# The first layer's MLP: half of its fc1 groups as block products (Strassen-Winograd), fc2 after every four fc1 tiles, side jobs moved forward

## The chip, the cores and the metric

The kernel runs on one core of a Trainium2 chip. The metric is the device time of one execution, in microseconds (us). TensorE (PE) multiplies, VectorE (DVE) and ScalarE (ACT) work element by element, GpSimd (POOL) does a few such operations, and SyncE (SP) sends most of the weight transfers.

## The reference

Two transformer-like blocks of two layers each, in float32. The part in question is the MLP of the first layer of the first block. It runs for 512 tokens and for 256 context tokens, with the same weights; the kernel does both as 768 columns.

```python
def _sq_relu_mlp(h, w1, w2):
    a = jnp.maximum(h @ w1, 0)
    return (a * a) @ w2
...
        x = _layer_norm(DEEPNORM_ALPHA * x + g2 * _sq_relu_mlp(h, w_fc1[l], w_fc2[l]), ln2_g[l], ln2_b[l])
```

D_MODEL is 1024 and the hidden size 4096. `g2` is one of six modulation vectors of a layer, a product of a condition with a 1024 x 6144 matrix.

## The kernel before, in words

Each engine has one queue of instructions, written out by hand in Python; what stands in it is done in that order, and semaphores tie the queues together. Activations lie with features on the partitions and tokens along the row.

**Precision by parts.** Every float32 matrix product is three matmuls: high weight by high operand, low weight by high operand, high weight by low operand. So each weight tile (128 x 1024, 512 KB) that has landed is split: ScalarE copies the high part (`act_split`, L590) and VectorE subtracts it (`dve_split`, L622). High parts have NS = 3 places, so the copy for tile a waits until TensorE is through with tile a - 3; landed tiles and low parts have a ring of NR = 4 slots. `act_tiles(key)` and `dve_tiles(key)` do the splits up to the tile two after `key`.

**The first layer's MLP** (`mlp`, `pe_mlp`, `act_mlp`, `dve_mlp`) has fc1 with 32 tiles of 128 hidden features and fc2 with 32 tiles too, in four rounds: eight fc1 tiles, then the eight output tiles of fc2 for these eight. A tile is 24 pairs of matmuls with 512 and 256 columns (`pe_dense`, L866 and L870), and goes in turn to one of two PSUM banks of 1024 columns, ps[0] and ps[1]. An fc1 tile is evicted in four steps: ScalarE's Relu (L1252, which frees the bank), VectorE's square (L1276), ScalarE's high part (L1254), VectorE's low part (L1279). An fc2 tile is added to the residual by VectorE (`dve_add_gated`, L924), which frees the bank.

**Jobs.** Beside this MLP the kernel makes the modulation vectors of the next two layers (`modulation`). It has 128 jobs, each a 512 KB tile of the modulation matrix in one of NM = 3 buffers, multiplied and summed on VectorE (L731), and four changes of condition (two transposes' banks copied by ScalarE, L721). They are dealt evenly over 64 steps, one step behind each tile; a step has two or three jobs. In ScalarE's queue a step is, for each job, a wait until VectorE has done it and the send (L691) that refills its buffer.

**The later MLPs** (`eighths`, `quarters`, with 512 tokens) already use block products. In `eighths` the hidden features come in eight groups of four tiles; the first is plain, the others are seven products of half size in place of eight (Winograd's form of Strassen). A product is 24 matmuls of 256 columns (L1378). VectorE also makes the sums of the weight blocks (L600) and of the products (L1546). The fc2 of each group follows it at once; a transfer tile of fc2 there holds two outputs of four blocks each, and its banks are four of 512 columns. The ring has XR = 4 more slots from the second layer's MLP on.

```python
                act_tiles((name, "evict", q, m) if e != 0 else fc1(name, 0, 1))
                ACTQ.wait_ge(*made(key))
```

These lines of `act_mlp` set which weight copies stand ahead of a tile's Relu; the mark ("evict", q, m) lies right behind tile m. In `act_eighths` it is

```python
                    act_tiles(fc1(name, 0, min(m + 2, 3)))
                    evict(m)
```

## Time and profile before

| | |
|---|---|
| median of 3 runs | 3000.74 us (2996.26 to 3006.47) |
| profiled execution, its own time | 3000.01 us |
| span of its trace | 2998.7 us |
| PE busy | 2843.8 us (95%) |
| DVE busy | 1877.8 us (63%) |
| ACT busy | 1197.6 us (40%) |
| POOL busy | 340.6 us (11%) |
| moved by DMA | 315.98 MB, mean 105 GB/s |

Each engine's busy time is given with its share of the span. PE runs nearly always, so the other engines matter where PE waits for them. The first layer's MLP takes the span's stretch from about 514 to 1070 us.

### The profile page before, as it was taken

The page shows a single profiled execution, that of the slowest core. Times are in us where ns is not written, and L with a number is a line of the kernel's source. Part 1 is how long each engine was busy: PE and PEld are TensorE (multiplying, and loading weights), DVE is VectorE, ACT ScalarE, POOL GpSimd, SP SyncE. Part 2 cuts the span into 40 slices and gives each one's busy share as a digit, 9 for nine tenths or more (in the row PEclk, how much of TensorE's full clock was granted, in tenths as well). Part 3 has the DMA queues.
Part 4 walks back from the last instruction along what each step waited for, and adds up shares of the span by engine and source line. Part 5 has one row for each costly group of instructions (what it writes and reads, how often), then busy time and mean ns, then how long its engine had stood idle before and what let it go on. Part 6 is the DMA issues. An engine that isn't in the chain of part 4 may idle for free. (4 is left out here: it accounts for less than half of the span.)

```text
span 2998.7 us, 43305 instructions
## 1 busy us (share of the span) xinstructions
PE 2843.8 (95%) x17474; PEld 2305.1 (77%) x17474; DVE 1877.8 (63%) x2790; ACT 1197.6 (40%) x1963; POOL 340.6 (11%) x371
## 2 busy tenths in 40 slices
PE   7999998999999989999899998998889999899998
PEld 6766667888888867766688886776667999678896
DVE  3656544656565646665687765646736788567765
ACT  4245443412122252554443555212643444344443
POOL 2022220300000030321301002000510000110000
PEclk9999999999999999999999999998999999999999
DMA  7222001556565511001232331322024555412331
GB/s 282 78 98 80 8 22 43 169 196 210 171 209 183 194 57 51 8 15 57 89 106 81 110 113 57 102 64 63 1 89 131 167 182 168 138 59 90 106 106 64
DMA packets 88495, 315.98 MB, mean 105 GB/s; under 512 B 9991, under 2 KB 12295, under 8 KB 88040
## 3 DMA queue, kind: packets, MB, share of 16 engines
q1 hardware_dynamic: 59040, 213.94, 22.3%
q10 hardware_dynamic: 29256, 99.26, 9.9%
q8 instruction: 140, 2.29, 0.3%
q14 instruction: 59, 0.48, 0.1%
HBM read 311.06 MB, written 2.10 MB: 104 GB/s over the span
## 5 line engine op out<-in xcount | busy, mean ns | idle before, releaser
L866 PE MATMUL bank<-t 128*128 128x512 f32 x4064 | 1011.0, 360 | 25.5 <-ACT t L1172 7.7
L866 PEld LDWEIGHTS bank<-t 128*128 128x128 f32 x4064 | 672.9, 190 | 164.4 <-issue 41.4
L590 ACT ACTIVATE t<-t 128x1024 fp32r<-128x1024 f32 x410 | 431.0, 1055 | 761.0 <-PE bank L870 263.9
L622 DVE TENSOR_TENSOR t<-t 128x1024 fp32r<-128x1024 f32 x410 | 508.3, 1243 | 332.3 <-ACT t L590 328.1
L870 PE MATMUL bank<-t 128*128 128x512 f32 x2032 | 607.6, 359 | 8.3 <-POOL t L1181 7.6
L870 PEld LDWEIGHTS bank<-t 128*128 128x128 f32 x2032 | 336.3, 190 | 73.7 <-POOL t L1181 11.9
L1399 PE MATMUL bank<-t 128*128 128x512 f32 x1024 | 309.6, 398 | 1.2 <-ACT t L1469 1.0
L1378 PEld LDWEIGHTS bank<-t 128*128 128x128 f32 x2352 | 281.4, 188 | 1.9 <-issue 0.8
L1378 PE MATMUL bank<-t 128*128 128x256 f32 x2352 | 282.0, 281 | 0.0
L1399 PEld LDWEIGHTS bank<-t 128*128 128x128 f32 x1024 | 190.8, 189 | 55.3 <-issue 5.7
L731 DVE SCALAR_TENSOR_TENSOR t<-t 128x1024 f32<-128x1024 f32 x176 | 209.3, 1222 | 4.6 <-DMA t<-in_mod 4.5
L1404 PE MATMUL bank<-t 128*128 128x512 f32 x512 | 187.4, 396 | 0.0
L1898 POOL TENSOR_SCALAR t<-t 128x768 f32<-128x768 f32 (+3 forms) x160 | 125.7, 788 | 522.0 <-DVE t L1866 522.0
L924 DVE SCALAR_TENSOR_TENSOR t<-bank,t 128x512 f32<-128x512 f32 (+1 forms) x128 | 81.5, 664 | 148.2 <-PE bank L870 131.0
L1697 PE MATMUL bank<-t 64*128 64x384 f32 (+2 forms) x768 | 136.9, 475 | 16.1 <-ACT t L1796 5.2
L1841 DVE TENSOR_REDUCE t<-bank 128x1 f32<-128x768 f32 (+1 forms) x120 | 96.6, 845 | 86.9 <-PE bank L1706 65.8
L1786 ACT ACTIVATE t<-bank 128x384 f32<-128x384 f32 (+1 forms) x160 | 73.6, 460 | 172.3 <-PE bank L1714 171.9
L1714 PEld LDWEIGHTS bank<-t 128*128 128x128 f32 x784 | 86.8, 142 | 58.2 <-issue 29.1
L1714 PE MATMUL bank<-t 128*128 128x128 f32 x784 | 121.9, 284 | 9.5 <-DVE t L1852 6.7
L1796 ACT ACTIVATE t<-bank,t 128x768 f32<-128x768 f32 (+3 forms) x160 | 124.1, 780 | 14.0 <-DVE t L1841 8.0
L992 ACT ACTIVATE t<-t 128x512 f32<-128x512 f32 (+1 forms) x64 | 43.8, 684 | 214.2 <-DVE t L924 132.6
L1592 DVE SCALAR_TENSOR_TENSOR t<-bank,t 128x512 f32<-128x512 f32 x128 | 93.5, 746 | 48.1 <-PE bank L1404 47.8
(363 smaller groups left out, 3385.3 us busy)
## 6 DMA issues: line engine op xcount, KB each, us to landing
t<-in_mod ACTq DMA_DIRECT2D x176, 512.0 KB, 4.3
t<-in_l0fc SPq DMA_DIRECT2D x64, 512.0 KB, 4.1
t<-in_l1fc SPq DMA_DIRECT2D x64, 512.0 KB, 3.6
t<-in_s0fc SPq DMA_DIRECT2D x64, 512.0 KB, 3.7
t<-in_s1fc SPq DMA_DIRECT2D x64, 512.0 KB, 3.6
t<-in_mod SPq DMA_DIRECT2D x48, 512.0 KB, 4.5
t<-in_mixin SPq DMA_DIRECT2D x24, 512.0 KB, 3.6
t<-in_l0in SPq DMA_DIRECT2D x12, 512.0 KB, 3.7
```

The costliest lines, as they stand in the source:

```text
L590: act.activation(high_of(key), landed_of(key), ACT.Copy).then_inc(*up("act_whi", a))
L622: dve.tensor_tensor(low_of(key), landed_of(key), high_of(key).bitcast(F32), ALU.subtract).then_inc(*up("dve_wlo", a))
L731: dve.scalar_tensor_tensor(x, x, 1.0, sil[:, :], ALU.mult, ALU.mult, accum_out=modt[L][:, j, s:s + 1]).then_inc(*up("dve_job", (name, n)))
L866: pe.matmul(acc.ap[:, o:o + m], w[:, ws], Hh[:, k, o:o + m], start=k == order[0] and w is hi, stop=False)
L870: ins = pe.matmul(acc.ap[:, o:o + m], hi[:, ws], Hl[:, k, o:o + m], start=False, stop=k == order[-1])
L1378: ins = pe.matmul(dst, w[:, ws], x, start=pair == 0 and k == 0 and w is hi and x is high, stop=pair == 1 and k == 3 and x is low)
L1399: pe.matmul(banks[s].ap, w[:, ws], Ah[:, k, :], start=first and w is hi, stop=False)
L1404: ins = pe.matmul(banks[s].ap, hi[:, ws], Al[:, k, :], start=False, stop=last)
L1697: ins = pe.matmul(places[side][:, 512 * r + o:512 * r + o + m], g["q"][side](c), g["k"][side][:, k0:k0 + m], start=r not in begun, stop=last)
L1714: ins = pe.transpose(turns[r].ap[:, P * b:P * b + P], p[:, P * i:P * i + P], mat("ident"))
L1796: act.activation(keys_of(p, g), scores_of(ps[side], g), ACT.Exp, bias=row[:, 7:8], accum_out=row[:, 3:4]).then_inc(*ps[side].freed((tag, u ...
L1898: pool.tensor_scalar(x, x, stat(u, side)[:, 7:8], 1.0, ALU.mult, ALU.mult).then_inc(*up("pool_prob", (tag, u, side)))
```

## The change

The function `mlp` with its three queues goes, and the first layer's MLP uses `eighths`, which now takes a number of plain groups G, the token ranges and jobs. G is 4 for this MLP and 1 for the two others that use it. The last four groups are block products: 24 matmuls of 384 columns each, with three banks of 1024 columns. Fc2 follows every four fc1 tiles. A weight tile of fc2 holds two outputs of four blocks. There are now eight rounds, and so twice as many additions to the residual. The jobs are dealt over 128 steps: 24 steps in each plain group (three behind each tile), 8 in each block group, behind the fc2 tiles alone. The four additional ring slots come with this MLP. In `s0` and elsewhere the functions are only renamed.

```diff
-                self.slot[key], self.slot_after[key] = NR + a - G, ("l1out", 1)
+                self.slot[key], self.slot_after[key] = NR + a - G, ("l0out", 1)
...
+PLAIN_GROUPS = {"l0": 4, "l1": 1, "s0": 2, "s1": 1}
...
-                pe_step, act_step, dve_step, pool_all = modulation(name, sb(s, [P, 1024]), jobs, 2, 62)
...
+                *steps, pool_all = modulation(name, sil, jobs, 2, 126)
...
+    PRODUCT_BANKS = {NT: (0, 1, 2, 3, 0, 2, 3), T: (2, 0, 1, 2, 1, 2, 0)}
+    OUT_BANKS = {NT: (1, 0, 2, 3), T: (1, 0)}
...
+    def steps_beside(G, Q, m):
+
+        return range(24 * Q + 3 * m, 24 * Q + 3 * m + 3)
+
+    def steps_behind(G, Q, j):
+
+        return range(24 * Q + 12 + 3 * j, 24 * Q + 15 + 3 * j) if Q < G else range(16 * G + 8 * Q + 2 * j, 16 * G + 8 * Q + 2 * j + 2)
...
             if j == 0:
                 for s in range(2):
                     PEQ.wait_ge(*banks[s].claim(out_of(name, Q, 2 * j + s)))
-                for ks in ((1, 3), (0, 2)) if Q else ((0, 1), (2, 3)):
+                for ks in ((1, 3), (0, 2)) if Q >= G else ((0, 1), (2, 3)):
...
+        places = {key: fours[m % 4] if n == NT else ps[m % 4 % 3] for m, key in enumerate(first)}
...
-            if Q == 0:
+            if Q < G:
                 for m in range(4):
-                    act_tiles(fc1(name, 0, min(m + 2, 3)))
-                    evict(m)
+                    act_tiles(fc1(name, 4 * Q + min(m + 2, 3)))
+                    evict(Q, m)
+                    if step:
+                        for s in steps_beside(G, Q, m):
+                            step(s)
...
-                act_tiles(fc2_pair(name, Q, j))
-                if Q == 0:
+                act_tiles(fc2(name, Q, j))
+                if Q == G - 1:
                     for t in ((0, 1), (2,), (3,), ())[j]:
                         operand_high(t)
+                if step:
+                    for s in steps_behind(G, Q, j):
+                        step(s)
...
+                if Q == 0:
+                    dve_tiles(fc1(name, 1))
+                    for t in range(4):
+                        operand(t)
                 for m in range(4):
-                    dve_tiles(fc1(name, 0, min(m + 2, 3)))
-                    evict(m)
+                    dve_tiles(fc1(name, 4 * Q + min(m + 2, 3)))
+                    evict(Q, m)
+                    if step:
+                        for s in steps_beside(G, Q, m):
+                            step(s)
```

How ScalarE's queue stands in an fc1 round of this MLP, away from its ends. L590 (L579 in the changed kernel) is a weight copy, L1252 (L1402) the Relu, L1254 (L1407) the high part, L691 (L680) the sends of jobs. Before, two tiles:

```order
L590 ACTIVATE t<-t 128x1024 [waits s_pe_tile,s_tile_in2]
L1252 ACTIVATE t<-bank 128x768 [waits s_pe_tile]
L1254 ACTIVATE t<-t 128x768 [waits s_dve_asq]
L691 DMA t<-in_mod 128x1024 [waits s_dve_job] x3
L590 ACTIVATE t<-t 128x1024 [waits s_tile_in3]
L1252 ACTIVATE t<-bank 128x768 [waits s_pe_tile]
L1254 ACTIVATE t<-t 128x768 [waits s_dve_asq]
L691 DMA t<-in_mod 128x1024 [waits s_dve_job] x2
```

In the changed kernel, the four fc1 tiles of plain group 1:

```order
L579 ACTIVATE t<-t 128x1024 [waits s_pe_tile,s_tile_in2]
L579 ACTIVATE t<-t 128x1024 [waits s_pe_tile,s_tile_in3]
L579 ACTIVATE t<-t 128x1024 [waits s_pe_tile,s_tile_in0]
L1402 ACTIVATE t<-bank 128x768 [waits s_dve_alo]
L1407 ACTIVATE t<-t 128x768 [waits s_dve_asq]
L680 DMA t<-in_mod 128x1024 [waits s_dve_job] x3
L579 ACTIVATE t<-t 128x1024 [waits s_pe_tile,s_tile_in1]
L1402 ACTIVATE t<-bank 128x768 [waits s_dve_alo]
L1407 ACTIVATE t<-t 128x768 [waits s_dve_asq]
L680 DMA t<-in_mod 128x1024 [waits s_dve_job] x3
...
L1402 ACTIVATE t<-bank 128x768 [waits s_dve_alo,s_pe_tile]
L1407 ACTIVATE t<-t 128x768 [waits s_dve_asq]
```

Three weight copies now stand ahead of a group's first Relu, one ahead of the second and none ahead of the other two; only the last Relu still has a wait of its own for TensorE.

TensorE's queue at the last fc1 matmuls of such a round and the first of fc2. Before:

```order
L870 MATMUL bank<-t 128x512
L870 MATMUL bank<-t 128x256
L866 MATMUL bank<-t 128x512 [waits s_ps1_read,s_act_ahi,s_dve_wlo,s_act_whi]
L866 MATMUL bank<-t 128x256
```

In the changed kernel:

```order
L859 MATMUL bank<-t 128x512
L859 MATMUL bank<-t 128x256
L1328 MATMUL bank<-t 128x512 [waits s_ps0_read,s_ps1_read,s_act_ahi,s_dve_wlo,s_act_whi]
L1328 MATMUL bank<-t 128x256
```

The first fc2 matmul waited for one bank, and now waits for two, ps[0] being the one that the group's fourth tile has just filled.

## Rows read from the trace of the kernel before

**Rows 1.** Stretches of 100 us: busy of each engine, granted clock, DMA share, GB/s.
```profile
600.00:700.00 100.00, 100.00 (x574) 87.28 (x573) 59.39 (x86) 20.92 (x22) 0.00 (x0) 1.00 0.61 197
...
900.00:1000.00 100.00, 100.00 (x573) 87.35 (x572) 60.68 (x83) 24.83 (x27) 0.00 (x0) 1.00 0.58 184
```
**Rows 2.** Waits of TensorE, 514 to 1050 us: total us, times, longest.
```profile
PE bank L866 <- ACT t L1172: 2.8, 1, 2.8
PE bank L870 <- POOL t L1181: 1.2, 1, 1.2
```
**Rows 3.** Timeline of VectorE, two additions: start, us, line, idle before and its releaser.
```profile
613.20 1.14 DVE L924 SCALAR_TENSOR_TENSOR t<-bank,t 128x512 f32<-128x512 f32 x2 [3.35 <-PE bank L870]
...
621.60 1.14 DVE L924 SCALAR_TENSOR_TENSOR t<-bank,t 128x512 f32<-128x512 f32 x2 [2.59 <-PE bank L870]
```
**Rows 4.** The chain that ended last, one block group of the last MLP.
```profile
2728.09 20.00 PE bank L1378 x168
```
**Rows 5.** Timeline of VectorE, one fc1 tile with three jobs.
```profile
582.23 0.96 DVE L1279 TENSOR_TENSOR t<-t 128x768 fp32r<-128x768 f32 x1 [0.91 <-ACT t L1254]
583.11 1.22 DVE L731 SCALAR_TENSOR_TENSOR t<-t 128x1024 f32<-128x1024 f32 x1
...
585.40 1.22 DVE L731 SCALAR_TENSOR_TENSOR t<-t 128x1024 f32<-128x1024 f32 x1
...
588.21 1.23 DVE L622 TENSOR_TENSOR t<-t 128x1024 fp32r<-128x1024 f32 x1 [1.58 <-ACT t L590]
589.35 0.95 DVE L1276 TENSOR_TENSOR t<-t 128x768 f32<-128x768 f32 x1
591.21 0.96 DVE L1279 TENSOR_TENSOR t<-t 128x768 fp32r<-128x768 f32 x1 [0.91 <-ACT t L1254]
```
**Rows 6.** Groups of instructions, 536 to 1036 us: busy, mean ns, idle before and releasers.
```profile
L731 DVE SCALAR_TENSOR_TENSOR t<-t 128x1024 f32<-128x1024 f32 x125 | 148.2, 1223 | 2.6 <-DMA t<-in_mod 2.5
...
L590 ACT ACTIVATE t<-t 128x1024 fp32r<-128x1024 f32 x60 | 63.5, 1061 | 272.9 <-PE bank L870 143.1 <-DVE t L731 129.3 <-issue 0.4
```
**Rows 7.** Timeline of ScalarE in the same tile.
```profile
587.04 1.06 ACT L590 ACTIVATE t<-t 128x1024 fp32r<-128x1024 f32 x1 [4.84 <-DVE t L731]
588.01 0.79 ACT L1252 ACTIVATE t<-bank 128x768 f32<-128x768 f32 x1
```
**Rows 8.** Timelines of ScalarE and TensorE, the second MLP's plain group.
```profile
1474.38 0.57 ACT L1464 ACTIVATE t<-bank 128x512 f32<-128x512 f32 x1
...
1477.02 0.58 ACT L1464 ACTIVATE t<-bank 128x512 f32<-128x512 f32 x1
...
1479.39 0.58 ACT L1464 ACTIVATE t<-bank 128x512 f32<-128x512 f32 x1
...
1481.53 1.67 PE L1399 MATMUL bank<-t 128*128 128x512 f32 x6 [1.03 <-ACT t L1469]
```
**Rows 9.** Timelines of ScalarE, VectorE and GpSimd, the stage's start.
```profile
514.10 19.49 ACT L1172 ACTIVATE t<-t 128x512 fp32r<-128x512 f32 x32 [4.64 <-DVE t L1124]
...
534.86 1.80 DVE L622 TENSOR_TENSOR t<-t 128x1024 fp32r<-128x1024 f32 x1 [8.30 <-ACT t L590]
...
535.58 15.15 POOL L1185 TENSOR_SCALAR t<-t 128x768 f32<-128x768 f32 x8
```
**Rows 10.** Timeline of VectorE, a late job and the norm's shifts.
```profile
1011.48 1.23 DVE L731 SCALAR_TENSOR_TENSOR t<-t 128x1024 f32<-128x1024 f32 x1 [1.22 <-DMA t<-in_mod]
...
1012.69 0.96 DVE L1009 TENSOR_TENSOR t<-t 128x768 f32<-128x768 f32 x1
1013.57 0.95 DVE L1011 TENSOR_TENSOR t<-t 128x768 f32<-128x768 f32 x1
```
**Rows 11.** DMA issues of the page: queue, count, size, median us to landing.
```profile
t<-in_mod ACTq DMA_DIRECT2D x176, 512.0 KB, 4.3
```
**Rows 12.** Timeline of TensorE after a wait, and the granted clock of the stretch around it.
```profile
1858.89 2.05 PE L866 MATMUL bank<-t 128*128 128x512 f32 x4 [6.58 <-DVE t L3419]
...
1855.00:1860.00 5.00, 1.11 (x3) 0.94 (x4) 2.63 (x4) 4.45 (x7) 2.54 (x2) 0.50 0.03 10
1860.00:1865.00 5.00, 5.00 (x13) 3.85 (x12) 1.52 (x4) 1.94 (x4) 4.64 (x8) 0.50 0.00 0
```

More of the change, by code:

```diff
@@ L287, in quarters_order, with mlp_order @@
     t.mark((name, "end"))
-def eighths_order(t, name):
+def mlp_order(t, name):
     t.tile((name + "fc1", 0))
     t.tile((name + "fc1", 1), 1)
-    for m in range(2, 4):
-        t.tile((name + "fc1", m))
     for Q in range(8):
-        if Q:
+        if Q < PLAIN_GROUPS[name]:
+            for m in range(0 if Q else 2, 4):
+                t.tile((name + "fc1", 4 * Q + m))
+        else:
             t.quad(name + "fc1", Q)
@@ L299, in eighths_order @@
             t.tile((name + "fc2", 4 * Q + j))
-    t.mark((name, "end"))
-def mlp_order(t, name):
-    t.tile((name + "fc1", 0))
-    t.tile((name + "fc1", 1), 1)
-    for q in range(4):
-        for m in range(NK):
-            if 8 * q + m > 1:
-                t.tile((name + "fc1", 8 * q + m))
-            t.mark((name, "evict", q, m))
-        for m in range(NK):
-            t.tile((name + "fc2", 8 * q + m))
     t.mark((name, "end"))
@@ L1305, in eighths @@
-    def eighths(L, name, N, after, centered, make_h, columns, beside=None, weights=None):
-        n, half = NT, 256
+        half = n // 2
         keys = [out_of(name, 7, m) for m in range(NK)]
@@ L1323, in eighths @@
             cells = modw[:, 0:2, :].rearrange("p a (b n) -> p (a b) n", b=2) if L == 1 else sb(S, [P, 4, n])[:, :, :]
-            M = Norm(after, LAT, [space[:, i, :] for i in range(4)], centered, updated_at(keys, after, centered), weights)
+            sil = sb(S, [P, 1024]) if jobs else None
+            M = Norm(after, ranges, [space[:, i, :] for i in range(4)], centered, updated_at(keys, after, centered), weights)
             begin_stage()
@@ L1398, in high @@
                 for w in (hi, lo):
-                    pe.matmul(banks[s].ap, w[:, ws], Ah[:, k, :], start=first and w is hi, stop=False)
+                    for o, m, _ in ranges:
+                        pe.matmul(banks[s].ap[:, o:o + m], w[:, ws], Ah[:, k, o:o + m], start=first and w is hi, stop=False)
             def low(s, k, last):
@@ L1403, in low @@
                 ws = slice(512 * s + P * k, 512 * s + P * k + P)
-                ins = pe.matmul(banks[s].ap, hi[:, ws], Al[:, k, :], start=False, stop=last)
+                for o, m, _ in ranges:
+                    ins = pe.matmul(banks[s].ap[:, o:o + m], hi[:, ws], Al[:, k, o:o + m], start=False, stop=last)
                 if last:
@@ L1443, in pe_eighths, with act_eighths @@
                     beside(4 * Q + j)
+                if step:
+                    for s in steps_behind(G, Q, j):
+                        step(s)
         pe_norm_step(M, 7, acc_of[keys[0]].after(keys[0]))
[L1445 to L1446 removed]
+        if n == NT:
+            for bank in fours:
+                PEQ.wait_ge(*bank.after(bank.order[-1]))
         pe_tiles((name, "end"))
[L1449 to L1450 removed]
+    def act_eighths(name, G, htag, n, Hh, Tr, T3, Th, Ah, cells, M, beside, step):
+        half = n // 2
         def operand_high(t):
@@ L2877, in pe_quads @@
             PEQ.wait_ge(*bank.claim((name, "quads")))
-        first = [fc1(name, 0, m) for m in range(NK)]
+        first = [fc1(name, m) for m in range(NK)]
         pe_dense(first[0:2], Hh, Hl, hh, hl, LAT, dict(zip(first, fours)))
```

448 lines of the change are left out of this document (185 added, 263 removed).

## The prediction

> **What bounds the kernel now.** I read the span and the stretches first. The core is in the first MLP from about 514 to 1070 us, and inside it TensorE has no free moment: 100.00 of 100 us busy in each stretch, at full clock [rows 1]. The list of waits says the same: from 514 to 1050 us TensorE waited twice, 4.0 us together, both at the stage's start [rows 2]. So this stage costs what its matmuls cost, and a cut in matmul columns comes out at the end as long as nobody makes TensorE wait. The question is whether VectorE and ScalarE keep ahead in the new order.
>
> One tile takes 8.40 us: two successive second-layer additions on VectorE, each started by the end of its tile, stand 8.40 us apart [rows 3]. It has 24 pairs of a 512- and a 256-column matmul, so 350 ns a pair. In the later block stage 168 matmuls of 256 columns take 20.00 us, 119 ns each [rows 4]. A 512-column one is then 231 ns, and a 384-column one, halfway, 175 ns; by the 256-column row times 1.5 it would be 179 ns at most.
>
> Then the other engines. One tile with three jobs on VectorE [rows 5]: low part, three jobs at 1.15 us, a wait of 1.58 us for ScalarE's weight copy, weight split, square, a wait of 0.91 us, low part. From one low part's start to the next are 8.98 us, against a tile of 8.40; with two jobs it is 7.83. It fits today because the mean is 2.2 jobs a tile. ScalarE is not busy but it is tied: of its idle time before weight copies 129.3 us end with a job of VectorE [rows 6], since in its queue the sends that refill the job buffers stand ahead of the copy and wait for the jobs. It comes to the weight copy at 587.04, 0.5 us after the third job, having idled 4.84 us [rows 7].
>
> **The change part by part.**
>
> Matmuls. Fc2 has the same matmuls in another order. Of fc1, four groups of four tiles (33.6 us each) become seven products of 24 matmuls of 384 columns: 7 x 24 x 0.175 = 29.4 us. Gain 4 x 4.2 = **16.8 us** (14.3 with 179 ns).
>
> Plain groups (the first four): the eviction comes late. The new queue of ScalarE puts three weight copies ahead of the first Relu of a group, and the third copy waits for the end of the group's second tile. Before, the Relu of a tile stood behind a copy that waits for the tile before. Everything below is counted from the end of the group before, TensorE being in time. Second tile ends 16.8; copy 16.9 to 18.0; VectorE split to 19.15; square; low part from 21.0 (1.86 after the square's start [rows 5]) to 21.9; three jobs, done at 25.3. Second eviction: its copy waits for the third tile (25.2), so split, square, low part and jobs as in [rows 5], 8.9 us, done 34.25. Third: no copy ahead, so Relu straight behind the sends (0.45 + 0.81, square from 1.33 after the jobs), then 1.86 + 0.88 + 3.44: 7.5 us, done 41.75. Now the fourth Relu ends at 43.05. It is what frees bank ps[0], in which the fourth tile lies, and the first fc2 tile claims ps[1] and ps[0] before its first matmul. TensorE was ready at 33.6: **it stands 9.5 us**. The fourth eviction and its jobs run to 49.3, split to 52.0, three more jobs to 55.5, and only then the addition (1.14) that frees ps[1] for the second fc2 tile: 56.7, where TensorE was ready at 51.5, another **5.2 us**. From there each fc2 tile gives VectorE split 1.14, jobs 3.44 and two additions 2.28 in 8.4 us, and it keeps up. The same kind of lateness is already in the trace of the second MLP, which has this order but no jobs and four banks: the last three Relus follow one another from 1474.38 to 1479.39, though their tiles end 5.6 us apart, and TensorE waits 1.03 us [rows 8].
>
> In groups 1 to 3 the first fc1 tile also claims ps[0], whose last user was added up only after its end: 1.14 + 0.1 = 1.25 us. So 15.95 x 3 = **47.9 us**. The job count is not always three: one set of four ahead of a fourth Relu and two changes of condition (ScalarE copies two banks, 1.06 us) there: **4.5 us**.
>
> Group 0 starts later still. VectorE has to make four operand differences of 1536 elements first, after ScalarE's last h (514.10 + 19.49, [rows 9]). By 1.23 us for 1024 and 0.96 for 768 elements [rows 5] each is 1.77 us; beside GpSimd's work the 1024-wide split took 1.80 instead of 1.23 [rows 9], and at that rate each is 2.6. They stand ahead of the first eviction. With the shorter price the fourth Relu ends 13.3 us after TensorE is ready, with the longer 17.5; with the second stall 18.7 or 22.9, I take the middle, **20.8 us**. The Trainium skill (page "SBUF — State Buffer", section "SBUF: two separate sides") says that a VectorE operation with two SBUF inputs and a GpSimd operation that reads SBUF lock each other out for whole instructions; by that rule the longer price holds and the term is 22.9. The trace agrees that the split is slower there, by half and not by a whole instruction.
>
> Group 3 carries the operands' high and low parts: four more VectorE operations of 1.77 us in three fc2 tiles that have 1.5 us to spare each, with two block sums (1.15): **4.3 us**.
>
> Block groups. Seven products of 4.2 us; VectorE has at most two sums (0.95 each, [rows 10]), a split and a low part in one, 4.1 us, so it keeps up. But with three banks two hand-overs lie bare: the sixth corner's sum stands between the last product and fc2 (1.1 us), and the first addition comes 1.1 us after the second fc2 tile could start. 2.2 x 4 = **8.8 us**.
>
> The last group feeds the norm. The second output's addition now waits for the shift sum, which TensorE does only after the third output, and the fourth output needs that bank: ScalarE copy 0.85, two shifts 0.95 each, addition 1.14 [rows 3, 10] and hand-over, 4.2 us, then 1.3 for the next: **5.5 us**. Before, two whole tiles lay between.
>
> Jobs and DMA: the same 128 transfers, 4.3 us to landing [rows 11], each sent three jobs ahead. In the tight part the first is wanted 6.4 us after it is sent, so hidden; late ones cost 1.2 us as now [rows 10]. Ring growth earlier: more weights ahead in the second layer; TensorE there doesn't wait for weight transfers, 0 to 3 us gained, taken as 0.
>
> Sum: -16.8 + 20.8 + 47.9 + 4.5 + 4.3 + 8.8 + 5.5 = **+75.0 us** on the profiled execution's 3000.01 us, 0.7 below the median of the three runs: 3075.
>
> **The rivals.**
> (a) My case, evictions held behind jobs: 3075. For it: the order, and the idle times of [rows 5, 7]. Its bounds: price of a 384-column matmul (+2.5), group 0 (+-2), and 2 us either way in each of eight stalls.
> (b) The first stall comes but the second doesn't, since VectorE gets through its jobs while TensorE stands: 75.0 - 4 x 5.2 = 54, 3054. Against it: the additions stand behind two sets of jobs in the queue.
> (c) The clock. TensorE idled 6.58 us before 1858.89 and was granted 0.50 in the 5 us around it; the first eight matmuls went at half rate, until about 1865 [rows 12]. That is the lower of its two levels, 1.2 GHz, for 6 us, 3 us lost. After a 9.5 us stall it will do the same, but these 3 us fall into the second stall, which shrinks from 5.2 to 2.2; I count nothing. If they don't, or fall again behind the second stall, 3 us in each of four groups, or 6: 3087 to 3099. The Trainium skill (page "TensorE: Matmul & The Clock Gate", section "HAM oscillation") has a kernel that falls back to the slow clock in every round because every round has such a gap; by it the 3 us are paid in each group, 3087.
> (d) The other side: only VectorE's rate decides, not its order. A plain group holds 25.5 jobs, 8 splits, 4 evictions, 8 additions: 29.3 + 9.1 + 7.4 + 9.1 = 55 us in 67.2. If the banks are handed over in time it is all hidden and the change gives its 16.8 us: 2983. It decides from the point where the fourth Relu ends by 33.6 instead of 43. The waits of [rows 5, 8] speak against it.
> (e) As (d), but the bank hand-overs at group borders stay: -16.8 + 3 x 1.25 + 8.8 + 5.5 = +1.3, no change.
>
> **How the numbers follow.** Chances: (a) 0.62, (b) 0.10, (c) 0.18, (d) 0.05, (e) 0.05. A measurement of this kernel tells about 0.3%, 9 us, from no change. (a), (b) and (c) are slower, so 0.90; same 0.05; faster 0.05. The range reaches from a little below (b), 3048, to near the top of (c), 3096; it leaves out (d), (e) and the tails.
>
> **What would show it.** TensorE idle before the first fc2 matmul of each of the first four groups by 8 to 18 us, released by ScalarE's Relu; before the second fc2 tile by 2 to 5 us, released by the addition; matmuls of 384 columns at 175 ns; block groups of 29.4 us with 1.1 us before fc2; a granted clock under 1 in the first half of the stage alone. VectorE idle for most of the first two tiles of a plain group. I am wrong if TensorE is busy through the first half, if the stalls are released by DMAs, or if the second half is where time is lost.

## The result, and the profile after

The changed kernel takes 3098.1 us (median of four runs, 3095.0 to 3100.4) against 2998.5 before: ratio 1.0329, interval 1.0316 to 1.0343. It is slower, by 100 us instead of the predicted 75, and 2 us above the predicted range. The profiled execution took 3100.2 us with a span of 3098.8.

The whole loss lies in the first MLP. The matmul that picks the norm's sums ends the stage; the timeline of TensorE has it, first in the kernel before, then in the changed one (start, us, line; the idle time before it in brackets):

```profile
1070.44 1.50 PE L1037 MATMUL bank<-t 128*128 128x2 f32 x12 [0.92 <-ACT t L1065]
```
```profile
1171.98 2.72 PE L1026 MATMUL bank<-t 128*128 128x2 f32 x12 [0.91 <-ACT t L1054]
```

That is 101.5 us later; what follows takes 1926.8 us instead of 1928.3. Stretches of the changed kernel, as in [rows 1]:

```profile
600.00:700.00 100.00, 82.05 (x449) 70.69 (x447) 62.96 (x96) 16.90 (x18) 0.00 (x0) 0.91 0.60 202
700.00:800.00 100.00, 80.62 (x430) 69.39 (x431) 54.89 (x82) 17.13 (x21) 0.98 (x5) 0.90 0.53 176
900.00:1000.00 100.00, 96.24 (x543) 88.43 (x542) 72.47 (x91) 37.26 (x42) 0.00 (x0) 1.00 0.41 127
```

Before, TensorE was busy for all of each such stretch and granted 1.00. In the first half it now idles a fifth of the time and its granted clock falls to 0.90; in the second half it idles 4% at full clock. The list of TensorE's waits from 500 to 1170 us, where [rows 2] had two waits (total us, times, longest):

```profile
PE bank L1328 <- ACT t L1402: 49.7, 4, 14.5
PE bank L1328 <- DVE t L1536: 29.4, 13, 4.5
PE bank L1328 <- DVE t L1490: 5.0, 4, 1.3
PE bank L957 <- ACT t L981: 4.5, 2, 3.4
PE bank L855 <- DVE t L1536: 3.2, 3, 1.4
PE bank L855 <- ACT t L1161: 2.9, 1, 2.9
```

L1328 is fc2's matmul and L1402 ScalarE's Relu: once in each plain group TensorE stands before the first fc2 tile, 12.4 us on average. L1536 is the addition, L1490 the product sum of the last corner, L981 the square of the norm. The timeline of TensorE in groups 1 and 2 shows the waits and what the matmuls behind them took; 16 of the L1328 rows' matmuls take 2.96 us at full rate, and four 0.86:

```profile
658.10 4.90 PE L1328 MATMUL bank<-t 128*128 128x512 f32 x16 [13.02 <-ACT t L1402]
...
664.24 2.96 PE L1328 MATMUL bank<-t 128*128 128x512 f32 x16
...
671.95 1.27 PE L1328 MATMUL bank<-t 128*128 128x512 f32 x4 [3.35 <-DVE t L1536]
...
673.66 1.48 PE L1328 MATMUL bank<-t 128*128 128x512 f32 x4
...
745.73 5.37 PE L1328 MATMUL bank<-t 128*128 128x512 f32 x16 [11.63 <-ACT t L1402]
...
772.38 1.62 PE L1328 MATMUL bank<-t 128*128 128x512 f32 x4 [3.65 <-DVE t L1536]
```

And the granted clock (column behind POOL) of two stretches of 5 us in group 1, the first in the long wait, the second around the short one:

```profile
655.00:660.00 5.00, 1.90 (x6) 1.64 (x7) 2.45 (x4) 1.65 (x2) 0.00 (x0) 0.50 0.84 297
...
670.00:675.00 5.00, 3.05 (x11) 2.65 (x12) 5.00 (x8) 1.06 (x1) 0.00 (x0) 0.73 0.95 365
```

So the clock falls to its lower level, 1.2 GHz, twice in the group: in the long wait, and again at the short one, though the matmuls from 664.24 on had run at full rate.

Why the Relu is late is in the timeline of VectorE (L720 a job, L1481 the square) and in ScalarE's row of the same Relu. The set of jobs ahead of the fourth Relu has four, and two of them wait for their transfers besides:

```profile
649.97 1.22 DVE L720 SCALAR_TENSOR_TENSOR t<-t 128x1024 f32<-128x1024 f32 x1
...
651.83 1.23 DVE L720 SCALAR_TENSOR_TENSOR t<-t 128x1024 f32<-128x1024 f32 x1 [0.63 <-DMA t<-in_mod]
...
655.33 1.23 DVE L720 SCALAR_TENSOR_TENSOR t<-t 128x1024 f32<-128x1024 f32 x1 [0.99 <-DMA t<-in_mod]
...
657.88 0.96 DVE L1481 TENSOR_TENSOR t<-t 128x768 f32<-128x768 f32 x1 [1.31 <-ACT t L1402]
...
657.03 0.81 ACT L1402 ACTIVATE t<-bank 128x768 f32<-128x768 f32 x1 [7.97 <-DVE t L720]
```

The block groups are nearly as predicted: 168 matmuls in 30.2 us in the first group and 29.9 us in the three others, a hand-over of 1.25 us, 65.7 to 66.1 us from one group to the next. TensorE's timeline in the first of them:

```profile
882.64 30.22 PE L1306 MATMUL bank<-t 128*128 128x384 f32 x168
914.12 2.27 PE L1328 MATMUL bank<-t 128*128 128x512 f32 x11 [1.25 <-DVE t L1490]
```

The last group takes 91.8 us. TensorE's waits in it, and VectorE's rows that end one of them: its split (L611) waits for ScalarE's copy, three jobs follow, and only then the addition for which TensorE stands:

```profile
1130.32 1.65 PE L1328 MATMUL bank<-t 128*128 128x512 f32 x4 [3.94 <-DVE t L1536]
...
1152.12 1.62 PE L1328 MATMUL bank<-t 128*128 128x512 f32 x4 [4.47 <-DVE t L1536]
...
1169.45 0.62 PE L957 MATMUL bank<-t 128*32 128x512 f32 x2 [3.39 <-ACT t L981]
...
1145.27 1.22 DVE L611 TENSOR_TENSOR t<-t 128x1024 fp32r<-128x1024 f32 x1 [6.41 <-ACT t L579]
...
1150.83 1.14 DVE L1536 SCALAR_TENSOR_TENSOR t<-bank,t 128x512 f32<-128x512 f32 x2
```

The balance of the stage: matmuls saved, 4 x 33.6 - 30.2 - 3 x 29.9 = 14.5; waits 91.8 instead of 2.0, +89.8; matmuls at half rate, from rows like those above, 21.9 (9.0 behind the four long waits, 7.6 behind the next one of each plain group, 5.3 in the last group). Together 97.2 of the 101.5. The rest is about what the stops cost beside the waits: in a stretch without gaps a row of two matmuls lasts 0.51 us and the next row begins after 0.35, and at each of the 26 stops this overlap of 0.16 us is missing, some 4 us. That is an estimate from these rows.

### The profile page after: what moved, and what is told of

Its sections match the earlier page's. It is cut to its first block, busy times and chain, and to the rows that moved or that the text cites. A ratio compares the mean times of both kernels' runs of the same rounds, so it can differ in the third digit from the quotient of the medians.

```text
span 3098.8 us, 43300 instructions
## 1 busy us (share of the span) xinstructions
PE 2854.7 (92%) x17378; PEld 2321.4 (75%) x17378; DVE 1968.7 (64%) x2902; ACT 1228.9 (40%) x1999; POOL 345.6 (11%) x371
## 4 chain that ended last, share of the span: by engine, by line
PE 51%; DVE 5%; ACT 3%; issue 2%; POOL 1%; ACTq 0%; DVEq 0%; POOLq 0%
PE bank L855 9%; PE bank L1306 8%; PE bank L1328 8%; PE bank L859 5%; PE bank L2810 4%; PE bank L1334 4%; PE bank L1648 2%; PE bank L3772 1%; PE bank L1665 1%; PE bank L1709 1%; PE bank L2140 1%; PE bank L3273 1%; ACT t L579 1%; DVE t L611 1%; PE bank L2535 1%
## 5 line engine op out<-in xcount | busy, mean ns | idle before, releaser
L579 ACT ACTIVATE t<-t 128x1024 fp32r<-128x1024 f32 x422 | 443.4, 1055 | 812.1 <-PE bank L1334 334.1
L611 DVE TENSOR_TENSOR t<-t 128x1024 fp32r<-128x1024 f32 x422 | 523.6, 1244 | 368.8 <-ACT t L579 364.8
L855 PE MATMUL bank<-t 128*128 128x512 f32 x2528 | 680.4, 374 | 30.7 <-ACT t L1161 7.8
L1328 PE MATMUL bank<-t 128*128 128x512 f32 (+1 forms) x2048 | 540.7, 378 | 85.7 <-ACT t L1402 49.7
L855 PEld LDWEIGHTS bank<-t 128*128 128x128 f32 x2528 | 438.4, 192 | 134.6 <-issue 43.0
L1328 PEld LDWEIGHTS bank<-t 128*128 128x128 f32 x2048 | 360.1, 196 | 171.4 <-issue 92.7
L859 PE MATMUL bank<-t 128*128 128x512 f32 x1264 | 410.8, 372 | 5.7 <-POOL t L1170 4.4
L1306 PE MATMUL bank<-t 128*128 128x256 f32 (+1 forms) x3024 | 402.2, 294 | 2.5 <-issue 2.4
L1306 PEld LDWEIGHTS bank<-t 128*128 128x128 f32 x3024 | 400.3, 188 | 5.0 <-issue 3.8
L1334 PE MATMUL bank<-t 128*128 128x512 f32 (+1 forms) x1024 | 314.6, 371 | 0.0
L859 PEld LDWEIGHTS bank<-t 128*128 128x128 f32 x1264 | 218.3, 191 | 56.0 <-POOL t L1170 11.6
L1536 DVE SCALAR_TENSOR_TENSOR t<-bank,t 128x512 f32<-128x512 f32 (+1 forms) x256 | 165.8, 680 | 82.1 <-PE bank L1334 81.1
L720 DVE SCALAR_TENSOR_TENSOR t<-t 128x1024 f32<-128x1024 f32 x176 | 208.4, 1221 | 12.9 <-ACT t L710 7.0
L1334 PEld LDWEIGHTS bank<-t 128*128 128x128 f32 x1024 | 176.5, 191 | 36.3 <-DVE t L1517 2.7
L1648 PE MATMUL bank<-t 64*128 64x384 f32 (+2 forms) x768 | 138.4, 479 | 16.5 <-ACT t L1747 5.0
L1665 PEld LDWEIGHTS bank<-t 128*128 128x128 f32 x784 | 86.4, 142 | 58.7 <-issue 32.1
L981 ACT ACTIVATE t<-t 128x512 f32<-128x512 f32 (+1 forms) x64 | 43.7, 684 | 205.5 <-DVE t L913 98.2
```

The costliest lines, as they stand in the source:

```text
L579: act.activation(high_of(key), landed_of(key), ACT.Copy).then_inc(*up("act_whi", a))
L611: dve.tensor_tensor(low_of(key), landed_of(key), high_of(key).bitcast(F32), ALU.subtract).then_inc(*up("dve_wlo", a))
L720: dve.scalar_tensor_tensor(x, x, 1.0, sil[:, :], ALU.mult, ALU.mult, accum_out=modt[L][:, j, s:s + 1]).then_inc(*up("dve_job", (name, n)))
L855: pe.matmul(acc.ap[:, o:o + m], w[:, ws], Hh[:, k, o:o + m], start=k == order[0] and w is hi, stop=False)
L859: ins = pe.matmul(acc.ap[:, o:o + m], hi[:, ws], Hl[:, k, o:o + m], start=False, stop=k == order[-1])
L1306: ins = pe.matmul(dst, w[:, ws], x, start=(pair == 0 or n > NT) and k == 0 and w is hi and x is high, stop=pair == 1 and k == 3 and x is l ...
```

## The experiments

Experiments 1 to 7 are the changed kernel with one part altered (3 has the narrow jobs of 2 as well, 7 alters the dealing of the jobs and the rhythm of the evictions); 8 to 11 put several cures together, and 12 alters the kernel before. Times are medians, ratios are to the kernel before beside them; line numbers move by a few where an edit adds lines. "Less" is against the changed kernel's 3098.1 us.

The kernel before took 2998.5 us beside the result and 2994.5 beside experiments 1, 2, 4 and 5, so their gains are 4 us smaller by the ratios. From the norm's row ahead of the stage to that at its end (L1026) the profiles are shorter by 20.1, 45.1, 17.8 and 25.2 us, which speaks for the medians.

**1. Evictions in the old rhythm.** In both queues:

```diff
-                    act_tiles(fc1(name, 4 * Q + min(m + 2, 3)))
+                    act_tiles(fc1(name, max(1, 4 * Q + m) if G == 4 else 4 * Q + min(m + 2, 3)))
```

> Evictions of the first four groups in the old rhythm: the Relu of tile m stands behind the weight copies that tile m's entry brings, no longer behind those of tile m+2. Jobs, banks and matmuls as in the change. Theory A (late first eviction plus jobs in VectorE's queue): evictions begin with the end of the first tile (8.4 us), go on at 8.98 us a set and the fourth Relu ends at about 36.3 us from the group's start instead of 43 to 48; the stall before fc2 falls from 10.5 to 14.5 us to about 3 (group 0: about 6), the second stall stays at 3 to 5: 35 us less in all, about 3063 us. Theory B (VectorE's amount of work decides, the order doesn't): the fourth Relu moves by less than 2 us and the time stays at 3090 to 3100.

3078.0 us, ratio 1.0274 (1.0245 to 1.0304): 20 us less, not 35. TensorE's waits at the first stall of each group:

```profile
559.95 1.62 PE L855 MATMUL bank<-t 128*128 128x512 f32 x4 [13.96 <-ACT t L579]
```
```profile
653.03 5.06 PE L1328 MATMUL bank<-t 128*128 128x512 f32 x16 [5.11 <-ACT t L1402]
...
733.59 5.46 PE L1328 MATMUL bank<-t 128*128 128x512 f32 x16 [4.02 <-ACT t L1402]
...
818.97 3.05 PE L1328 MATMUL bank<-t 128*128 128x512 f32 x16 [2.43 <-ACT t L1402]
```

In groups 1 to 3 the first stall is 2.4 to 5.1 us, about as theory A had it; these groups give 22 us together. In group 0 the cure is the illness: the weight copy (L579) of the fourth tile now stands behind two evictions, which wait for VectorE's operands, and two sets of jobs. So group 0 got 3 us longer; the expectation had its stall fall to 6 us. The second stalls stayed, at 2.7 to 6.5 us.

**2. Jobs with an eighth of VectorE's work.** L720 over 128 of 1024 columns in this MLP, 0.29 us instead of 1.22; seven eighths of each dot product are left out:

```diff
-                    x = modw[:, n % NM, :]
+                    x, w = modw[:, n % NM, :], 128 if name == "l0" else 1024
...
-                    dve.scalar_tensor_tensor(x, x, 1.0, sil[:, :], ALU.mult, ALU.mult,
+                    dve.scalar_tensor_tensor(x[:, 0:w], x[:, 0:w], 1.0, sil[:, 0:w], ALU.mult, ALU.mult,
```

> The first MLP's jobs multiply 128 of the 1024 columns on VectorE (7/8 of each modulation dot product is left out); their transfers, ScalarE's sends and every wait stay. Theory A: a job falls from 1.15 us to about 0.3, nine of them stand ahead of the fourth Relu and six to nine between it and the first addition, so the first stall falls by 7.6 us to about 3 to 6 and the second vanishes; 45 us less, about 3053. Rival (the jobs' transfers or ScalarE's queue hold the evictions, not VectorE's time): less than 15 us of the 98 go, 3083 or more. Rival (late order alone, jobs innocent): first stalls stay above 8 us.

3052.9 us, ratio 1.0190 (1.0159 to 1.0222): 45 us less, as theory A says. But the first stalls are 10.6, 8.1, 5.9 and 5.4 us, not 3 to 6; in groups 0 and 1 they stay above 8 us, as the rival with the late order alone had it. The second stalls fall to 0.6 to 0.9 us. VectorE's timeline ahead of the first stall of group 1:

```profile
641.54 0.29 DVE L720 SCALAR_TENSOR_TENSOR t<-t 128x128 f32<-128x128 f32 x1 [0.81 <-DMA t<-in_mod]
...
644.52 0.29 DVE L720 SCALAR_TENSOR_TENSOR t<-t 128x128 f32<-128x128 f32 x1 [2.68 <-DMA t<-in_mod]
...
646.13 0.96 DVE L1481 TENSOR_TENSOR t<-t 128x768 f32<-128x768 f32 x1 [1.31 <-ACT t L1402]
```

As soon as VectorE's time goes, the transfers (4.5 us each, three buffers) hold the last set. VectorE's time and the transfers are two limits close behind each other.

**3. The transfers made small too** (the narrow jobs, and only the first 128 columns of each job's buffer filled).

> As the narrow jobs, and each job's transfer brings 128 of the 1024 columns too (an eighth of the bytes, same number of transfers and waits; 7/8 of each dot product left out). With narrow jobs alone the first stalls were 10.61, 8.14, 5.86 and 5.39 us and VectorE's third set of jobs waited 0.81 and 2.68 us for transfers in group 1. Theory A (the sets stand so close behind the late evictions that three buffers and a transfer of 4 us hold the last set): those waits go where a short transfer lands sooner, the first stalls of groups 1 to 3 fall by 2 to 3.5 us to about 4 (what the late order costs without jobs), about 3043 us. Rival (a small transfer takes as long to land as a large one, the latency is fixed): stalls as with narrow jobs, 3050 or more.

A transfer of 64 KB lands in 2.0 us (median) instead of 4.5. The first stalls are 10.0, 6.1, 4.8 and 5.0 us, so the transfers had cost 2.0, 1.0 and 0.4 in groups 1 to 3, and some 5 us are what the late order costs without any jobs in the way. 3053.1 us, ratio 1.0185 (1.0164 to 1.0205): on the total nothing gained over 3052.9, as the rival had it, though its reason, a transfer that lands no sooner, is wrong. The profiled stage ends 5.3 us earlier than with narrow jobs alone, but it had begun 3.6 us earlier, and waits that had been harmless there are followed by matmuls at half rate here (last section). The two runs of each kernel lie 5 to 6 us apart, so the runs can't tell what small transfers are worth.

**4. Three banks for fc2's outputs**, in all groups but the last:

```diff
-    OUT_BANKS = {NT: (1, 0, 2, 3), T: (1, 0)}
+    OUT_BANKS = {NT: (1, 0, 2, 3), T: (2, 1, 0)}
...
+            order = OUT_BANKS[n] if n == NT or Q < 7 else (1, 0)
```

> Groups 0 to 6 put the eight fc2 outputs into banks 2, 1, 0, 2, 1, 0, 2, 1 instead of 1, 0, 1, 0; the last group keeps 1, 0. Nothing else moves. Theory A (the claim of ps[0] and ps[1] is what TensorE waits for): the stall at the first fc2 tile shrinks by 3 to 5 us, since 14 of its 24 pairs of matmuls can go before the fourth tile's high part, and its releaser becomes ScalarE's copy; the second stall goes; the 1.25 and 0.63 us hand-overs of groups 1 to 6 go. 4 x 7 + 3 x 1.25 + 3 x 1.9 = 37 us less, about 3061. Rival (the data of the fourth eviction, not the bank, is what comes late): the first stalls only move behind the 14 pairs at full length less 1 us and the additions stay late; only the hand-overs go, 10 us, about 3088.

3081.9 us, ratio 1.0287 (1.0257 to 1.0317): 16 us less, between the theories. TensorE in group 1, and at the first block product:

```profile
645.95 4.59 PE L1329 MATMUL bank<-t 128*128 128x512 f32 x16 [2.33 <-issue]
658.49 4.21 PE L1329 MATMUL bank<-t 128*128 128x512 f32 x12 [5.85 <-ACT t L1408]
```
```profile
871.56 8.76 PE L1306 MATMUL bank<-t 128*128 128x384 f32 x39 [8.71 <-DVE t L1537]
```

The first stall is cut in two, 2.3 and 5.9 us instead of 13.0, the second part waiting for data (L1408, the fourth tile's high part). The hand-overs of the block groups are gone. But VectorE is no earlier: TensorE still waits 7.0 us for an addition in group 0 and 6.2 in group 2, and 8.7 us before the first product, a place where it did not wait with two banks.

**5. Jobs ahead of evictions** in groups 1 to 3, 6, 3, 3, 0 instead of 3, 3, 3, 3 behind them:

```diff
+        if Q and G == 4:
+            return range(24 * Q + (0, 6, 9, 12)[m], 24 * Q + (6, 9, 12, 12)[m])
...
+                    if step and Q:
+                        for s in steps_beside(G, Q, m):
+                            step(s)
                     act_tiles(fc1(name, 4 * Q + min(m + 2, 3)))
                     evict(Q, m)
```

> Groups 1 to 3: the twelve jobs beside fc1 stand ahead of evictions as 6, 3, 3, 0 instead of behind them as 3, 3, 3, 3, so six fill VectorE's idle time in the first two tiles. Group 0 as in the change. Theory A: the fourth Relu ends about 4.4 us earlier, the first stalls of groups 1 to 3 fall to 6 to 9 us, the second stalls go (three jobs less ahead of the addition): 3 x 8 = 24 us less, about 3074. Rival (transfers: three buffers, 4.3 us a transfer, so that six jobs in a row take 10 us or more and hold ScalarE's copies back): no gain, TensorE waits for a weight copy in the second tile, 3095 or more.

3074.3 us, ratio 1.0262 (1.0232 to 1.0292): 24 us less, as theory A has it. TensorE:

```profile
652.67 4.51 PE L1330 MATMUL bank<-t 128*128 128x512 f32 x16 [7.44 <-ACT t L1404]
```
```profile
753.85 0.94 PE L1330 MATMUL bank<-t 128*128 128x512 f32 x4 [3.65 <-DVE t L1541]
...
755.13 1.48 PE L1330 MATMUL bank<-t 128*128 128x512 f32 x4
```

The first stalls are 7.4, 5.0 and 5.0 us in groups 1 to 3, the second ones 0.63 each; the wait of 3.65 us before the third fc2 tile of group 2 is the same as in the changed kernel. The work is the same and only its place differs: 24 us of the plain groups' loss come from where VectorE's work stands and not from its amount.

**6. The last group's order.** Output 0 to its end before output 1, the shift sum behind output 1, additions ahead of jobs and splits (part of the edit):

```diff
+                late = Q == 7 and G == 4
+                if not (late and j):
+                    dve_tiles(fc2(name, Q, j))
...
+                if late and j:
+                    dve_tiles(fc2(name, Q, j))
+                if step and late:
+                    for s in steps_behind(G, Q, j):
+                        step(s)
```

> Only the last group is changed: its first fc2 tile does output 0 to the end before output 1, the shift sum follows output 1 instead of output 2, and VectorE and ScalarE put their jobs (VectorE also the weight splits of tiles 1 to 3) behind the additions instead of ahead of them. Theory A (the last group's waits of 3.94, 4.47 and 3.39 us and the half-clock matmuls behind them come from what stands ahead of the additions): the first two waits fall under 1.5 us each, the clock stays at 1.00 there, 1.5 us are paid for the corner's data ahead of output 0; the first half is untouched: 10 us less than the change, about 3088. Rival (the norm's own chain sets the pace, the waits only move): 3 us or less, 3095 or more.

3081.6 us, ratio 1.0275 (1.0255 to 1.0296): 16.5 us less. None of the last group's waits on additions is over 0.8 us, the one before the sums falls from 3.39 to 1.11, and the group takes 74.6 us instead of 91.8. The cause stands; I had expected 10 us, since I had not counted that the matmuls at half rate (5.3 us) go with the waits.

**7. Jobs dealt so that they fit in the plain groups**, old rhythm of evictions from group 1 on. Steps beside the four fc1 tiles and behind the four fc2 tiles of each group:

```diff
+    BESIDE = [(0, 0, 0, 0)] + [(2, 2, 2, 2)] * 3 + [(0, 0, 0, 0)] * 4
+    BEHIND = [(3, 3, 3, 3)] + [(3, 4, 3, 4)] * 3 + [(4, 3, 4, 3)] * 3 + [(3, 3, 1, 1)]
```

> Jobs and evictions ordered so that neither stands in the way, two banks kept. Group 0: no job beside fc1, 3 behind each fc2 tile. Groups 1 to 3: the Relu of a tile stands right behind the tile, 2 jobs beside each fc1 tile, 3, 4, 3, 4 behind the fc2 tiles. Block groups: 14, 14, 14 and 8 jobs. Theory A (order, and VectorE's 55 us of work fit into 67): a set of eviction, split and two jobs takes 7.8 us, under the tile's 8.4, so the fourth Relu ends 1.3 us after its tile: groups 1 to 3 cost 67.2 + 5 us instead of 90 to 92, group 0 loses nine jobs (10 us) ahead of its fourth Relu: 11 + 3 x 18 to 19 = 67 us less, about 3032. Rival (VectorE's work decides): six jobs more in each block group and no idle time used show up as stalls there, 3060 or more.

3096.4 us, ratio 1.0324 (1.0304 to 1.0345): nothing gained, worse than its rival. The first stalls did what theory A said, 3.6, 1.2, 1.1 and under 0.8 us, and the block groups begin at 847.0 instead of 882.6 us. But the plain groups 1 to 3 took 77.6, 85.4 and 85.0 us and not the expected 72: TensorE now stands before additions there, 4.2 and 4.5 us in group 1, 3.9, 2.5 and 3.2 in group 2, 6.3 and 3.4 in group 3. Then the fc2 parts of successive block groups begin 75, 79 and 74 us apart instead of 65.7. VectorE and TensorE in one of them:

```profile
965.00 1.23 DVE L720 SCALAR_TENSOR_TENSOR t<-t 128x1024 f32<-128x1024 f32 x1 [1.23 <-DMA t<-in_mod]
...
968.51 1.23 DVE L720 SCALAR_TENSOR_TENSOR t<-t 128x1024 f32<-128x1024 f32 x1 [2.28 <-DMA t<-in_mod]
...
969.66 2.19 DVE L1542 SCALAR_TENSOR_TENSOR t<-bank,t 128x512 f32<-128x512 f32 x4
```
```profile
970.95 1.62 PE L1334 MATMUL bank<-t 128*128 128x512 f32 x4 [7.58 <-DVE t L1542]
```

Four steps hold five jobs here: that many in a row outrun the three buffers, and the addition stands behind them. From 540 to 1120 us VectorE waits 20.1 us for job transfers, in the changed kernel 5.8. So the block groups do not bear 14 jobs in this form; with 11, in experiment 10, they wait less. That they need as few as the change's 8 is not shown.

**8. The dealt jobs with three banks**, and **9. with the last group's order too.**

> As the dealt jobs, and in groups 0 to 6 the fc2 outputs go round three banks (2, 1, 0). Theory A: with VectorE in time the three banks do what they couldn't do beside late evictions: the 1.3 and 2.3 us waits of groups 1 to 3, the 1.25 us hand-overs and the 1.25 + 0.63 us of each block group but the last go: 3 x 5 + 3 x 1.9 + some 3 in group 0 = 24 us less than the dealt jobs with two banks, about 3008. Rival (as when the banks were tried alone, the waits gather at the border to the block groups because VectorE's operands and block sums of group 3 come late there): 10 us less, about 3022.

> Dealt jobs, three banks and the last group's order together. Theory A (the terms add): 3008 less the 10 us of the last group = about 2998: the 16.8 us of saved matmuls against some 5 us in group 0, 4 in group 3 and 4 to 5 in the last group, 0 to 8 us under the kernel before. Rival (each cure leaves VectorE a little later at the next place): 3010 or more, slower than before.

3061.6 us, ratio 1.0208 (1.0188 to 1.0229), and 3047.6 us, ratio 1.0169 (1.0152 to 1.0186). 35 us less than the dealt jobs with two banks (24 expected), then another 14 (10 expected): the two cures do more than I had set, but from 3096 and not from 3032, and both times stay far above what theory A had (3008 and 2998). With all three, group 0 and the first plain groups hardly wait any more. 46.9 us of waits are left in the stage, 43.4 of them on additions, 7.3 us of it before the first product and 2.5 to 3.4 at each later border of a block group.

**10. Fewer jobs behind the outputs**, and those of BESIDE ahead of each eviction:

```diff
+    BESIDE = [(0, 0, 0, 0)] + [(6, 2, 2, 2)] * 3 + [(0, 0, 0, 0)] * 4
+    BEHIND = [(4, 4, 4, 4)] + [(3, 3, 3, 3)] * 2 + [(3, 2, 2, 1)] + [(3, 3, 3, 2), (3, 3, 3, 2), (3, 3, 3, 2), (3, 3, 3, 2)]
```

> As all three together, with the jobs dealt otherwise: group 0 none beside fc1 and 4 behind each fc2 tile; groups 1 to 3 six ahead of the first eviction and two ahead of each other one; behind the fc2 tiles 3, 3, 3, 3 in groups 1 and 2 and 3, 2, 2, 1 in group 3; the block groups 11 instead of 14 (last 11). What the runs before showed: with 14 jobs each block group lost about 9 us, with 8 it lost 1.9. Theory A (VectorE idles in the first fc1 tile of a plain group and has no slack behind four jobs on an fc2 tile): the block groups' stalls fall to 1 to 2 us each (25 us less), the 7.3 us at the border to the blocks to 3, and six jobs in a row end before the first tile does not matter: about 3015. Rival (six jobs in a row wait for their transfers, and hold the first eviction and the fourth Relu): group 1 to 3 lose 3 us or more each and the time stays above 3030.

3028.8 us, ratio 1.0105 (1.0088 to 1.0121), the best full version, and still slower than before. Waits in the stage are 28.5 us and it ends at 1091.0 us, 20.5 after the kernel before, having begun 2.8 us earlier. The longest single wait is new: 5.5 us at 610.96, before the second fc1 tile of group 1. The row itself names no releaser, but VectorE's timeline shows what stands ahead of the tile's weight split at 609.64: from 590 to 608 it waits five times for a job's transfer, 0.91, 1.77, 2.27, 0.87 and 0.21 us. On this point the rival was right. Over the stage such waits are 24.5 us. The profiled execution took 3016.5 us, the three others 3026 to 3032; where those lost 10 to 15 us more I could not see.

**11. All three cures and narrow jobs.**

> As all three together, and the first MLP's jobs multiply 128 of 1024 columns on VectorE (7/8 of each dot product left out). It asks what the new order of matmuls is worth once VectorE is nearly free. Theory A (the 47 us that are left above the kernel before are VectorE's): nearly all stalls go, the 16.8 us of saved matmuls come out less 1 to 2 us in group 0 and 5 in the last group: 2985 to 2992. Rival (the transfers of the jobs or the clock hold something by themselves): above 3005.

2999.9 us (median of eight), ratio 1.0000 (0.9989 to 1.0010). Its stage ends at 1070.06 us, against 1070.44. The waits of TensorE in it, 520 to 1071 us:

```profile
PE bank L1335 <- DVE t L1556: 4.1, 3, 1.8
PE bank L1312 <- DVE t L1556: 3.3, 2, 2.7
PE bank L957 <- ACT t L981: 1.1, 1, 1.1
```

With VectorE's share of the jobs nearly gone this order is a tie: the products take 29.8 us a group (15 us saved in all), the waits come to 10.9 us instead of 2.0, and the other 6 us are matmuls at half rate, 1.7 us in the first products and 1.7 behind the wait at 782.15, and what I did not trace. Theory A (2985 to 2992) is out, its rival (above 3005) too.

That does not show what the order can give at best, for the jobs' transfers kept their full size here. VectorE waits 65.7 us for them in the stage, and such a wait stands right ahead of four of TensorE's: 3.21 us ahead of its 1.77, 0.50 and 2.48 ahead of its 2.67, 3.16 and 0.96 ahead of its 0.76, 6.06 ahead of its 1.55. These four and the matmuls at half rate are some 10 us, an estimate of the most that small transfers could bring. All three cures with narrow jobs and small transfers were not tried. One such pair, on VectorE and TensorE:

```profile
797.75 0.29 DVE L720 SCALAR_TENSOR_TENSOR t<-t 128x128 f32<-128x128 f32 x1 [2.48 <-DMA t<-in_mod]
...
799.25 31.52 PE L1312 MATMUL bank<-t 128*128 128x384 f32 x168 [2.67 <-DVE t L1556]
```

**12. The kernel before with narrow jobs.**

> The kernel before with the same narrow jobs in its first MLP (7/8 of each dot product left out): the measure for the run that had all three cures and narrow jobs. Theory A: TensorE never waits there, so the jobs are hidden and their width doesn't show: within 3 us of the kernel before; the new order without VectorE's load (2999.9) is then a tie with the old one, its saved matmuls being given back in its own waits. Rival (VectorE's load costs the old order something too): 2990 or less, and then the new order is worse even with free jobs.

2998.0 us, ratio 1.0000 (0.9991 to 1.0010): the jobs were hidden in the old order.

## Why the prediction was right or wrong

**Right: direction, place and mechanism.** TensorE stands before the first fc2 tile of each plain group until the Relu has freed ps[0], and before the second until an addition has freed ps[1]; experiments 1, 2 and 5 between them move both of these waits by moving or shortening what stands ahead. Rivals (d) and (e), that only VectorE's rate decides, are out, though the estimate of 55 us of work in a plain group was good (52.5 to 56.0 us busy in groups 1 and 2): experiment 5 does the same work in another place and gets 24 us back. Rival (b) is out too, the second stall came in every group.

**Matmuls**, predicted -16.8: -14.5. The 384-column matmul took 178 to 180 ns and not 175; the 256-column row times 1.5, which I had kept as the other end, was right.

**Group 0**, predicted 20.8: 22.1 (73.3 us from the end of the first two tiles instead of 51.2). That it comes so near is in part luck: the two stalls were 14.5 and 5.1 us, 1.2 less than the sum, and 1.7 us of matmuls at half rate behind the second one, which it had at nothing, made up for it. The four operand differences took 8.26 us (VectorE, from 536.65) where 7.1 and 10.4 were the ends. This bears on the rule of the Trainium skill (page "SBUF — State Buffer", section "SBUF: two separate sides"): it gave 22.9, but the operands' own rate lies between the free one and the one that the rule was read to mean.

**Groups 1 to 3**, predicted 47.9 + 4.5 + 4.3 = 56.7: 71.2 (90.0, 92.2 and 90.6 us against 67.2 each). Taken apart by the prediction's own steps:

- First stalls: 13.0, 11.6 and 10.5 us, 35.2 together, against 28.5 and the 4.5 for uneven sets. Right but for 2 us. VectorE waited for transfers in the sets ahead of the fourth Relu, 0.63 and 0.99 us in group 1 and 0.41 in group 3, which is the same 2 us. I had judged them hidden because the first job of a set is wanted 6.4 us after it is sent. In the tight part a set of four meets three buffers, and the fourth job's transfer is sent only when the first job is done.
- Second stall, from the start of the first to the start of the second fc2 tile, less the 8.4 us of a tile: 5.4, 5.1 and 6.3, against 5.2. Right, and with it the step that let the half-rate matmuls fall into the stall: 2.1 to 2.6 us of each are matmuls at half rate.
- Hand-overs: 1.4, 0.45 and 1.3 us against 3 x 1.25. Right.
- What comes behind: 16.0 us against 4.3. Here the prediction failed. It said "From there ... it keeps up", and counted 4.3 us for group 3. There were a third wait of 3.65 us in group 2 and two of 1 us in group 3. And in each group the clock falls a second time, 6.0 us in the three. Another 2.9 us are the transposes for three changes of condition (L689), which the kernel before makes too, 0.8 us each; by that much, 2.4 us, the miss here is smaller and that of the last group larger.

The third wait of group 2 is not a lack of time on VectorE, which idles for 5.40 us ahead of it. A change of condition falls there: TensorE makes the transposes only behind its second fc2 tile, ScalarE copies them (L710), VectorE's next job needs the copy, and the addition for which TensorE then stands is behind this job. The prediction had priced a change of condition at ScalarE's 1.06 us and had not followed this circle. Experiment 5 has the same 3.65 us. TensorE, then VectorE:

```profile
767.69 1.04 PE L689 MATMUL bank<-t 128*128 128x128 f32 x8
...
769.94 1.23 DVE L720 SCALAR_TENSOR_TENSOR t<-t 128x1024 f32<-128x1024 f32 x1 [5.40 <-ACT t L710]
```

**The clock** is the step that failed most: "I count nothing". It cost 12.9 us that the sum did not have, 7.6 behind the next waits of the plain groups and 5.3 in the last group. To count nothing was right behind the first stall and wrong behind the second, the case that the prediction kept as rival (c), 3087 to 3099, with a chance of 0.18. The measured 3098.1 lies there. The Trainium skill (page "TensorE: Matmul & The Clock Gate", section "HAM oscillation — how this bites in real kernels") describes a kernel that pays the slow clock anew in every round. The trace agrees, with two falls a plain group; by the half-rate rows it is 21.9 us in the stage, of which the sum had about 9 inside its second stalls and nothing for the rest. By that rule the prediction had written 3087: nearer, and still short.

**The last group**, predicted 2.2 + 5.5 on top of its share: 91.8 us, 8.7 more than the sum gives it. The first wait was set right (3.94, with 4.2 counted). The second was set at 1.3 and was 4.47, since I had not followed VectorE's queue: its weight split waits for ScalarE, which stands at a square, and three jobs stand between split and addition. The third, 3.39 before the last sums, I had not counted at all, nor the half rate behind the first two. Experiment 6 takes 17.2 us away from this group.

**Block groups**, predicted 65.2 each: 65.7 to 66.1. **Ring growth**, taken as 0: what follows the stage took 1926.8 instead of 1928.3 us, and 1921 to 1931 in all the experiments on the changed kernel, so nothing that can be seen. It was not tried alone: the block groups need the larger ring.

Sum of the misses: 1.3 + 14.5 + 1.9 (three block groups) + 8.7 = 26.4, and 75.0 + 26.4 = 101.4 of the stage's 101.5. The range was too narrow on its upper side: its top should have carried the clock in the last group too.

## What to carry to other kernels

A stage whose matmuls run without a gap pays for every wait put into it twice, in the wait and in the half-rate matmuls behind it; here 92 us of waits brought 22 of these. Side work that hides well when each step of it stands behind one tile stops hiding when fewer banks or a burst of evictions make the same queue punctual: follow each engine's queue to its next releasing instruction, and count it as late as everything ahead of it. And before tuning a new order, take the side work nearly away in a trial, its transfers too: experiment 11 left them at full size, so that its tie does not tell what the order could give.

## What the runs showed of the hardware

The length of a wait alone doesn't tell whether the clock falls. Before the third fc2 tile of group 2 experiments 2 and 3 both wait 2.71 us, behind the same work. In experiment 2 the matmuls go on at full rate, granted 1.00 from 740 to 755 us. In experiment 3 they fall to half rate about a microsecond after they have begun again, granted 0.66 from 740 to 745. The wait and the second row of four behind it, in experiment 2 and in experiment 3:

```profile
748.57 0.94 PE L1328 MATMUL bank<-t 128*128 128x512 f32 x4 [2.71 <-DVE t L1536]
...
749.70 0.86 PE L1328 MATMUL bank<-t 128*128 128x512 f32 x4
```
```profile
740.59 0.98 PE L1329 MATMUL bank<-t 128*128 128x512 f32 x4 [2.71 <-DVE t L1537]
...
741.96 1.48 PE L1329 MATMUL bank<-t 128*128 128x512 f32 x4
```

Nor does it need a long wait or another one shortly ahead. In experiment 11 a wait of 1.77 us at 782.15 was followed by half rate (1.34 and 1.48 us for the next two rows of four), with no wait over 0.7 us in the 236 us before it; in experiment 7 one of 3.16 us at 765.08 was followed by full rate. What decides is not shown by these runs.

The row of the wait doesn't tell it either. In experiment 5 the four matmuls right behind the 3.65 us took 0.94 us, nearly full rate, but the next rows of four 1.48 and 1.39 us, and the clock granted from 755 to 760 us was 0.68. In the changed kernel, after the same 3.65 us at 772.38, already the first four took 1.62 us. Read the rows of the two or three microseconds behind a wait before calling it harmless.

A job transfer of 512 KB landed in 4.5 us and one of 64 KB in 2.0 us, medians of 176 and 128 issues: an eighth of the bytes still takes 44% of the time.
